# The RWKV chunk loop on all four 64x64 pieces of TensorE, with four whole transpositions ahead of each level's first products

## What is computed

```python
def step(s, inp):
    r_t, w_t, k_t, v_t, a_t, b_t = inp
    sa = jnp.einsum('bhij,bhj->bhi', s, a_t)
    s = s * w_t[:, :, None, :] + sa[..., None] * b_t[:, :, None, :] + v_t[..., None] * k_t[:, :, None, :]
    return s, jnp.einsum('bhij,bhj->bhi', s, r_t)

s_fin, y = lax.scan(step, s0, xs)
```

## Time and profile before

| | us |
|---|---|
| median of 3 runs (2244.4 to 2256.14) | 2246.53 |
| the profiled execution | 2258.54 |
| its span, first to last instruction | 2256.7 |
| TensorE busy (23004 passes) | 1723.5 (76%) |
| TensorE weight loads | 1326.5 (59%) |
| VectorE busy | 622.6 (28%) |
| ScalarE busy | 375.9 (17%) |
| GpSimd busy | 185.2 (8%) |
| mean granted TensorE clock | 0.886 of full |

### The profile page before, as it was taken

The page is one execution under the profiler, slowest core; times in us unless marked ns, Lnnn a source line. Parts: engine busy times, 40 slices in busy tenths (PEclk is TensorE's granted clock), DMA queues, the critical chain, the costliest instruction groups (busy, mean ns, idle before and its releaser), DMA issues. The chain is left out here.

```text
span 2256.7 us, 51177 instructions
## 1 busy us (share of the span) xinstructions
PE 1723.5 (76%) x23004; PEld 1326.5 (59%) x23004; DVE 622.6 (28%) x1552; ACT 375.9 (17%) x893; POOL 185.2 (8%) x166
## 2 busy tenths in 40 slices
PE   3999679998043991699995399999999814999990
PEld 2788559997032571466663276788787612666660
DVE  3100342222735116111113501000363150121117
ACT  0300312222002003011111110000363120111112
POOL 1000022220000002100002200000000030000004
PEclk7999989999576796799997599899999957999995
DMA  6020060000230115699994522444211254999953
GB/s 190 19 75 19 0 262 5 4 4 9 81 114 24 38 56 193 255 382 385 388 384 147 154 31 74 127 103 102 63 62 58 75 220 152 366 393 388 370 214 139
DMA packets 218752, 345.62 MB, mean 153 GB/s; under 512 B 69673, under 2 KB 116433, under 8 KB 218282
## 3 DMA queue, kind: packets, MB, share of 16 engines
q1 hardware_dynamic: 191354, 289.04, 36.2%
q0 software_dynamic: 9856, 33.81, 4.8%
q10 hardware_dynamic: 17328, 19.51, 2.6%
HBM read 295.53 MB, written 46.78 MB: 152 GB/s over the span
## 5 line engine op out<-in xcount | busy, mean ns | idle before, releaser
L1713 PE MATMUL bank<-ring_extra,xT 128*32 128x256 f32 x3456 | 194.7, 379 | 9.1 <-issue 9.1
L2107 PE MATMUL bank<-x,ring 128*128 128x256 f32 (+1 forms) x768 | 174.4, 388 | 3.5 <-issue 2.7
L422 PE MATMUL bank<-mix,ring 128*128 128x260 f32 x768 | 172.9, 386 | 4.2 <-issue 3.1
L1713 PEld LDWEIGHTS bank<-ring_extra,xT 128*32 128x32 f32 x3456 | 135.7, 110 | 63.9 <-issue 17.4
L422 PEld LDWEIGHTS bank<-mix,ring 128*128 128x128 f32 x768 | 146.1, 191 | 31.0 <-issue 8.8
L2107 PEld LDWEIGHTS bank<-x,ring 128*128 128x128 f32 x768 | 146.3, 192 | 28.3 <-issue 5.5
L1713 PE MATMUL bank<-ring,xT 128*32 128x256 f32 x2688 | 156.5, 387 | 7.3 <-issue 6.0
L1713 PEld LDWEIGHTS bank<-ring,xT 128*32 128x32 f32 x2688 | 102.0, 112 | 57.3 <-issue 16.2
L1505 DVE TENSOR_TENSOR sg<-sg,bank 128x128 f32<-128x128 f32 x96 | 27.3, 285 | 379.3 <-ACT sg L1602 379.3
L1802 PE MATMUL bank<-ring,x 128*128 128x256 f32 (+1 forms) x480 | 108.2, 386 | 2.5 <-PEq L2292 1.3
L1802 PEld LDWEIGHTS bank<-ring,x 128*128 128x128 f32 (+1 forms) x480 | 82.4, 174 | 28.4 <-issue 7.4
(11 more groups left out here) (363 smaller groups left out, 2556.3 us busy)
## 6 DMA issues: line engine op xcount, KB each, us to landing
ring_extra<-in_moe_w_gate SPq DMA_DIRECT2D x72, 512.0 KB, 9.7
ring_extra<-in_moe_w_up SPq DMA_DIRECT2D x72, 512.0 KB, 12.9
ring_extra<-in_moe_w_down SPq DMA_DIRECT2D x36, 1024.0 KB, 15.1
ring<-in_moe_w_gate SPq DMA_DIRECT2D x56, 512.0 KB, 9.6
ring<-in_moe_w_up SPq DMA_DIRECT2D x56, 512.0 KB, 12.5
ring<-in_moe_w_down SPq DMA_DIRECT2D x28, 1024.0 KB, 14.3
ring<-in_a_w_rkv SPq DMA_DIRECT2D x12, 1024.0 KB, 5.1
xe<-expert_in POOLq DMA_DIRECT2D x32, 384.0 KB, 7.7
```

The lines of the kernel that those rows point to most:

```text
L422: ins = pe.matmul(ps[2 * (job % 4) + h][:, 0:HALF], w[:, kt, q * 128:(q + 1) * 128], m[:, kt, h * HALF:(h + 1) * HALF], start=kt == 0, sto ...
L1713: ins = pe.matmul(ps[i % 2][32 * q:32 * q + 32, 0:256], xT[:, kt, 32 * u:32 * u + 32], gate_up(w[kt // 2], kt % 2, q), start=kt == 0, stop ...
L2107: ins = pe.matmul(ps[2 * (job % 3) + h][:, 0:n], w[:, kt_, rr, :], z[:, kt_, lo:lo + n], start=kt_ == 0, stop=kt_ == 7)
```

## The change

A product may now have its input in one half of the partitions and its output in the other. The two heads of a pair (hp) and the parity of the pair (p2) take those parts, so the sixteen products of a step go over all four 64x64 pieces of the array in the order of `quads`; each row half writes its own PSUM bank. Tiles have two layouts: by pair (heads in partition halves) and by quad (parity in partition halves), and a transposition of 128x128 turns one into the other.

- The halves b are gone. A level is `turn_t` (four 128x128 transpositions), `solve_x` (16 products), one filler step, `solve_d` (16 products), another filler step. `mask` and `add` are two VectorE instructions each, as before, but both wait for all sixteen products; `copy_t` is one ScalarE instruction of 128x256 (128x512 at level 1, which had none).
- Scores: B and K meet A and R, which lie side by side (AR), in one product of 128 moving columns (`scores_b`, `scores_k`); `scores_n` stays at 64. The state step likewise: `state_v` and `state_m` give W and the early part of Y together. `out_u` is separate, and VectorE adds it (`sum_y`). W is turned once more (`turn_w`).
- Transpositions of V, B and K are four full ones each instead of 16 products each. The level-0 T and its turning are gone: GpSimd forms Tt from the masked score (one instruction instead of two), and copies V (`VS`).
- Products a chunk: 304 of 64x64, 64 of them with 128 moving columns, and 36 transpositions, instead of 480.
- The table of constants grows from 1884 to 1948 columns.

The core of the diff (the functions of TensorE, its order, and VectorE's):

```diff
+    QUADS = PAIRS // 2
     with ExitStack() as own:
...
+                quads = [(q, p2, hp) for q in range(QUADS) for p2, hp in ((0, 0), (1, 1), (0, 1), (1, 0))]
...
+                def solve_x(k, l):
...
+                        pe.wait_ge(tt_new, 2 * (5 * k + l - 1))
+                    for q, p2, hp in quads:
+                        ins = pe.matmul(ps[p2][rows[hp], 32 * q:32 * q + 32], N[k % 2][rows[p2], hp, q], blocks(Tt[k % 2][rows[p2], q, hp], l, 1),
+                                        start=True, stop=True)
+                    ins.then_inc(x_ready, 1)
+
+                def turn_t(k, l):
...
+                    for q in range(QUADS):
+                        ins = pe.transpose(ps[2][:, 128 * q:128 * q + 128], Tt[k % 2][:, q], ident)
+                    ins.then_inc(t_turned, 1)
+
+                def solve_d(k, l):
+                    pe.wait_ge(x_masked, 2 * (5 * k + l))
+                    pe.wait_ge(t_copied, 5 * k + l)
+                    for q, p2, hp in quads:
+                        ins = pe.matmul(ps[hp][rows[p2], 256 + 32 * q:288 + 32 * q], T[rows[hp], 2 * q + p2], X[rows[hp], p2, q], start=True, stop=True)
+                    ins.then_inc(d_ready, 1)
+
+                def scores_n(c):
...
+                    for q, p2, hp in quads:
+                        p = 2 * q + p2
+                        ins = pe.matmul(ps[3 + hp][rows[p2], 64 * q:64 * q + 64], AR[c % 4][rows[hp], p, 0], B[c % 2][rows[hp], p], start=True, stop=True)
+                    ins.then_inc(n_ready, 1)
+
+                def scores_b(c):
+                    pe.wait_ge(n_copied, 2 * c + 2)
+                    for q, p2, hp in quads:
+                        p = 2 * q + p2
+                        ins = pe.matmul(ps[3 + hp][rows[p2], 128 * q:128 * q + 128], B[c % 2][rows[hp], p], AR[c % 4][rows[hp], p], start=True, stop=True)
+                    ins.then_inc(bs_ready, 1)
+
+                def scores_k(c):
+                    pe.wait_ge(bs_copied, 2 * c + 2)
+                    for q, p2, hp in quads:
+                        p = 2 * q + p2
+                        ins = pe.matmul(ps[3 + hp][rows[p2], 128 * q:128 * q + 128], K[c % 2][rows[hp], p], AR[c % 4][rows[hp], p], start=True, stop=True)
+                    ins.then_inc(ks_ready, 1)
+
...
+                def state_v(c):
...
+                        pe.wait_ge(m_sum, 2 * c)
+                    pe.wait_ge(v_copied, c + 1)
+                    pe.wait_ge(ks_copied, 2 * c + 2)
+                    for q, p2, hp in quads:
+                        ins = pe.matmul(wy[p2][rows[hp], :, q], V[c % 3][rows[p2], q, hp], KS[c % 2][rows[p2], hp, q].rearrange("p (e t) -> p e t", e=2),
+                                        start=q == 0, stop=False)
+                    ins.then_inc(vk_done, 1)
+
+                def state_m(c):
+                    pe.wait_ge(vk_done, c + 1)
                     pe.wait_ge(m_new, c + 1)
-                    products(bank(4), ((A[c % 4], M), (KA[c % 2], V[c % 3])), True, True).then_inc(w_ready, 1)
+                    for q, p2, hp in quads:
+                        p = 2 * q + p2
+                        ins = pe.matmul(wy[p2][rows[hp], :, q], M[rows[hp], p], AR[c % 4][rows[hp], p], start=False, stop=q == QUADS - 1)
+                    ins.then_inc(wt_ready, 1)
+
+                def turn_w(c):
+                    pe.wait_ge(wt_copied, 2 * c + 2)
+                    if c:
+                        pe.wait_ge(u_copied, c)
+                    for q in range(QUADS):
+                        ins = pe.transpose(ps[7][:, 128 * q:128 * q + 128], WT[:, 2 * q:2 * q + 2], ident)
+                    ins.then_inc(w_ready, 1)
 
...
+                    pe.wait_ge(tt_new, 10 * c + 10)
+                    for q in range(QUADS):
+                        for hp in range(2):
+                            for p2 in range(2):
+                                at_u = 256 * hp + 64 * q
+                                ins = pe.matmul(ps[7][rows[p2], at_u:at_u + 64], Tt[c % 2][rows[p2], q, hp], W[rows[p2], q, hp], start=True, stop=True)
+                    ins.then_inc(u_ready, 1)
+
+                def out_u(c):
                     pe.wait_ge(u_copied, c + 1)
-                    products(bank(4), ((Bt[c % 2], U), (Kt[c % 2], V[c % 3])), True, True).then_inc(m_ready, 1)
-
-                def out_late(c):
-                    products(bank(5), ((U, BR[c % 3]),), False, True).then_inc(y_ready, 1)
+                    pe.wait_ge(y_first, 2 * c + 2)
+                    for q, p2, hp in quads:
+                        ins = pe.matmul(wy[p2][rows[hp], 0, q], U[rows[p2], hp, q], BS[c % 3][rows[p2], hp, q, 64:128], start=True, stop=True)
+                    ins.then_inc(y_ready, 1)
+
+                def add_m(c):
+                    pe.wait_ge(y_copied, 2 * c + 2)
+                    pe.wait_ge(kt_copied, c + 1)
+                    for q in range(QUADS):
+                        for i in range(2):
+                            for p2, hp in ((0, 0), (1, 1), (0, 1), (1, 0)):
+                                left, right = ((Bt[c % 2], U[rows[p2], hp, q]), (Kt[c % 2], V[c % 3][rows[p2], q, hp]))[i]
+                                ins = pe.matmul(wy[p2][rows[hp], 0, q], left[rows[p2], q, hp], right, start=q == 0 and i == 0, stop=q == QUADS - 1 and i == 1)
+                    ins.then_inc(m_ready, 1)
...
                 warm(8)
-                for k in range(-1, CHUNKS + 1):
-                    chain, state, prep = 0 <= k < CHUNKS, k >= 1, k + 1 < CHUNKS
+                scores_n(0)
+                warm(3)
+                scores_b(0)
+                warm(3)
+                scores_k(0)
+                turn_v_b(0)
+                for k in range(CHUNKS + 1):
+                    chain, state, prep = k < CHUNKS, k >= 1, k + 1 < CHUNKS
                     for l in range(1, 6):
-                        for b in range(2):
-                            if chain:
-                                solve_x(k, l, b)
-                                if l > 1:
-                                    turn_t(k, l, b)
+                        if chain:
+                            turn_t(k, l)
+                            solve_x(k, l)
+                        if chain and l == 1:
+                            turn_k(k)
+                        if state and l == 2:
+                            turn_w(k - 1)
+                        if state and l == 3:
+                            state_u(k - 1)
+                        if state and l == 4:
+                            out_u(k - 1)
+                        if state and l == 5:
+                            add_m(k - 1)
+                        if chain:
+                            solve_d(k, l)
                         if state and l == 1:
-                            pe.wait_ge(ka_copied, k)
-                            pe.wait_ge(v_copied, k)
-                            state_w(k - 1)
-                        if state and l == 2:
-                            state_u(k - 1)
+                            state_v(k - 1)
+                            state_m(k - 1)
                         if prep and l == 2:
-                            turn_v(k + 1)
-                        if state and l == 3:
-                            pe.wait_ge(bk_copied, 2 * k)
-                            state_m(k - 1)
-                        if state and l == 4:
-                            out_late(k - 1)
-                        for b in range(2):
-                            if chain:
-                                solve_d(k, l, b)
-                        if prep and l == 1:
-                            scores_a(k + 1)
-                        if state and l == 2:
-                            pe.wait_ge(kr_copied, k)
-                            out_early(k - 1)
+                            scores_n(k + 1)
                         if prep and l == 3:
-                            scores_r(k + 1)
+                            scores_b(k + 1)
                         if prep and l == 4:
-                            turn_t0(k + 1)
+                            scores_k(k + 1)
                         if prep and l == 5:
-                            turn_bk(k + 1)
-                        if k < 0 and l in (1, 3):
-                            warm(3)
+                            turn_v_b(k + 1)
 
...
+                def sum_y(c):
+                    dve.wait_ge(y_ready, c + 1)
+                    for p2 in range(2):
+                        y = f["w"][:, p2:PAIRS:2, at(c)]
+                        dve.tensor_tensor(y, wy[p2][:, 0], y, ALU.add).then_inc(y_copied, 1)
...
+                    for p2 in range(2):
+                        m = M[:, p2:PAIRS:2]
+                        dve.tensor_tensor(m, piece(5 + p2, 0, 64), m, ALU.add).then_inc(m_sum, 1)
...
+                    chain, state, prep = k < CHUNKS, k >= 1, k + 1 < CHUNKS
                     for l in range(1, 6):
```

(24 more changed lines are left out.)

349 lines of the change are left out of this document (140 added, 209 removed).

## The result

| | before | changed |
|---|---|---|
| median of the runs | 2248.76 us (4 runs, 2244.4 to 2256.14) | 2187.51 us (4 runs, 2182.13 to 2190.7) |
| ratio | | 0.9722, 95% interval 0.9688 to 0.9756 |
| profiled execution, span | 2258.54, 2256.7 | 2186.08, 2184.3 |

What follows compares the result with a forecast made beforehand. The loop was taken as bound by TensorE's rate of passes, 28.8 ns each. Loop -68.3, start -3.5 and tail +2.4 make -69.4: from a median of 2246.5 to 2177 us, range 2155 to 2212 (8 in 10).

Steps and rivals of the forecast that it cites:

- Bound and rate: Loop: bound by TensorE's rate of passes, 28.8 ns each; on four pieces 14.6 ns, with 29 as the no-gain bound.
- rival A: Groups on four pieces: 25 ns is a floor per pass; +4 us a chunk, 32 in all, 2209 us; chance 0.15.
- Levels: Five levels a chunk: own work 1.68 us each, 8.4 together, plus gaps of 11.0; a middle chunk is 19.6 us.
- four groups of 128 columns at 0.9: Score and state steps: 16 products with 128 moving columns, on four pieces, take 0.9 us a group.
- Mask and add in the open: Each level: the gap from a group's last pass to the next dependent one, 0.81 us, shows unless a filler covers it.
- The loop: All eight chunks: 17.4 + 6 x 19.6 + 18.7 = 153.7 us instead of 222, a gain of 68.3.
- TensorE waits for none of them: Loop: SP and its 28 DMAs are unchanged and cost TensorE no waiting; no time was put on them.
- nothing else counts in it: Loop before the change: 960 passes of 29 ns are 27.9 us a chunk against 27.7 measured, so the sum closes.
- Start and tail: Before the loop: it begins at 315 instead of 318.6 us, -3.5; the chain after the last level gets 2.4 longer.
- B: Pieces sharing rows or columns take turns, the rate stays 29 ns; +67 us in all, 2244, no change; chance 0.08.
- C: A load does not run beside a product in its own rows; 46 ns a pass, +15 us a chunk, 2297; chance 0.06.
- D: Loop: TensorE less busy, clock falls to 1.2 GHz; +18 us a chunk, all eight give 2315; chance 0.03.

Runs made afterwards that it cites:

- the fillers: Changed kernel plus one full-array product of 256 columns in each gap of the first chunk, into a bank nobody reads: 2186.98 us, ratio 0.9732 to the kernel before.
- the order within four: Changed kernel with the four pieces in another order within each four products, same rows next to each other: 2195.12 us, ratio 0.9763 to the kernel before.

## Why the prediction held, step by step

- **Bound and rate.** Right. The pass price of 14.6 ns is met (57 ns a round of four), with nothing for filling (0.46 from group to group, not 0.52). It rests on the step "each piece has its own 58", and the runs fit the mechanism behind it: a piece with its own queue, 58 ns a pass. L2004's 8.8 ns, the row I trusted against rival A, pointed the right way.
- **Levels.** Forecast 4.52, 3.33, 3.71, 3.79, 4.26 = 19.6; undisturbed 5.47, 3.14, 3.47, 3.50, 3.90 = 19.48. The sum is right by two errors that cancel. The step "four groups of 128 columns at 0.9" counted state_m among groups on four pieces. It uses two: +0.8, and it waits 0.33 for the last product of state_v, which I had not written down. On the other side stand a change between full and 64-wide products that costs a little less (0.17 on the way to the 64-wide ones; on the way back 0.17 behind 128 moving columns and 0.04 behind fewer), no filling, and a level 5 that is 0.36 shorter than worked out (its add_m starts 1.54 into the level, not 1.68, and ends at 2.47, not 2.66). That these cancel is luck.
- **Mask and add in the open.** Right in kind: 0.24 to 0.26 for X, 0.25 for Tt, longest at level 5 on y_copied, there 0.40. Not every level shows such a wait.
- **The loop, 153.7 forecast, 161.7 measured.** This is where the 8 us of difference lie, and it is outside the 150 to 158 us given as a sign of being right. By place: first chunk 21.9 instead of 17.4 (+4.5), k = 1 to 6 together 119.8 instead of 117.6 (+2.2), k = 7 20.0 instead of 18.7 (+1.3). The first chunk's step summed levels at full clock and without DMA traffic. The runs showed 2.7 us for half clock (21.9 to 19.2 with the fillers), and 2.7 us (19.2 to 16.5) for the filling transfers, which I had read only as "TensorE waits for none of them". That sentence is the step that failed: SP's data are waited for by nobody, yet they hold up TensorE. Each 2.7 is the difference of one pair of traces: by the other traces without fillers (19.8 to 21.2) the first is 0.6 to 2.0, by those with them (18.3 to 19.8) the second is 1.8 to 3.4. The stops in the kernel before, 1.30 and 1.14 us long while the transfers ran, would have told me; "nothing else counts in it" passed over them. Less than forecast, 16.5 against 17.4, is the chunk itself. The rest is the stops of the later chunks, open in their cause.
- **Start and tail.** 315.25 for 315, and +2.3 for +2.4. Only the tail says much: with the same code the loop began between 313.8 and 318.7 in other traces, so the start's quarter of a us is luck.
- **Rivals.** A (25 ns floor) and B (taking turns, 29 ns) fall by a round of four in 57 ns. The Trainium skill's floor of 25 ns (TensorE: Matmul & The Clock Gate, Part 1, "Wait — 56ns, not 53.3ns?") would have made 0.8 of each 0.42 from first to last load and is not what this trace shows for pieces. C falls with the order within four. B's 29 ns did appear, where only two pieces have work: state_u, and state_m with twice the columns. D (half clock) came in one chunk of eight, at +2.7 us instead of +18, since the stretch lasted only 13.7 us and the copies and masks between the groups don't slow down with it (L766 takes 279 to 294 ns in the whole loop, L843 384 or 385). I had it at 0.03 for the whole, and had not put its small form into the forecast.

## To carry to other kernels

Count a group of small products by its busiest piece of the array, not by its passes: 58 ns a pass and piece up to 64 moving columns here, some 104 at 128, whatever the other pieces do. List for each group which pieces its operands' rows and its output's rows leave it, and deal the products round in turn: two of a piece in a row cost 1.5 us in this loop, four in a row made a middle chunk of 31.5 us out of 20. Where TensorE issues passes at 14 ns, look for "issue" stops inside its groups and at what the DMA engines do meanwhile, even if nobody waits for those transfers.

## What the hardware showed that I had not expected

- Pieces of the array behave as if each took its passes from a queue of its own, about three passes deep: four passes of a piece in a row cost next to nothing (0.59 for 0.56), eight make a group of 1.18 out of 0.42. A later group starts on a free piece before an earlier one has started its last product on another (L704 at 409.88, L606 at 410.05).
- Transfers of constants that nobody reads here lengthen TensorE's stream: 2.7 us in the first chunk, and 8.7 us (21.7 + 26.1 against 19.5 + 19.6, a stretch of 3.4 us at half clock included) when moved into k = 1 and k = 2, with single stops up to 2.05 us.
- TensorE's clock fell to 0.50 in a stretch in which it was busy 12.16 of 13.7 us, right behind one busy 4.26 of 5.5. With 17.88 of 20 us busy it stayed at 1.00, and also with 13.82 of 20 in the version with another order within four, where it fell at 336.7, 1.7 us behind that stretch. How long the low stretch lasts differs between executions of like kernels (3.4, 6.8 or 13.7 us).
- An order of products that leaves the time of each group alone, two in a row at 0.59 for 0.56, made the middle chunks k = 2 to 5 steadier (20.21 to 20.22) than the order of the changed kernel does (19.48 to 20.58), at 163.2 us instead of 161.7 for the loop. Why is open.
